# Two of the first four ada_w blocks as rows on TensorE, parameter loads between chunks, gate steps laid out anew, last squares summed on VectorE

## The chip, the cores and the metric

The kernel runs on one core of a Trainium2 chip, all in fp32. The metric is the device time of one execution in microseconds (us), as the median of several runs. The engines are named as in the profile: PE (TensorE matmul), PEld (its weight load), DVE (VectorE), ACT (ScalarE), POOL (GpSimd), SP (SyncE, which only issues DMAs here). An fp32 matmul stands in the trace as two records.

## The reference

One sequence of 256 tokens, width 1024, runs through two layers. Everything is modulated by a vector `c`.

```python
cond = silu(c)
for l in range(2):
    mod = cond @ ada_w[l] + ada_b[l]           # ada_w[l]: 1024 x 9216; nine vectors of 1024
    sh0, sc0, gt0, sh1, sc1, gt1, sh2, sc2, gt2 = split(mod, 9)
    h = rms_norm(x, norm_g[l, 0]) * (1 + sc0) + sh0
    x = x + 0.5 * (1 + gt0) * swiglu(h, ffn_w_in[l, 0], ffn_w_out[l, 0])     # hidden width 2816
    h = rms_norm(x, norm_g[l, 1]) * (1 + sc1) + sh1
    x = x + (1 + gt1) * token_mixer(h, ...)    # RWKV-7 and mLSTM branches of 512 each, two sigmoid gates of 1024
    h = rms_norm(x, norm_g[l, 2]) * (1 + sc2) + sh2
    x = x + 0.5 * (1 + gt2) * swiglu(h, ffn_w_in[l, 1], ffn_w_out[l, 1])
return rms_norm(x, final_g)
```

## The kernel before

The program has five hand-written instruction streams, one for each engine, and each stream is executed in its order. Streams wait for one another through counters: `PE.at(l, "name")` is the count that PE's stream has reached when the step of that name is done, and DV, AC and PO are the same for DVE, ACT and POOL. So the order of the code is the order of the work, and a wait holds up everything behind it on its engine.

**Start.** SP loads `x` and the six units 2 to 7 of the first four column blocks of `ada_w[0]` (512 columns each, a block is two units of 1 MB, `ada_first`, L434); POOL loads units 0 and 1. PE transposes `x`, sums its squares with a matrix of ones, and computes block 1 of `cond @ ada_w` (units 2 and 3) as 32 matmuls with 128x128 weights and one moving column. DVE computes blocks 0, 2 and 3 with eight multiply-adds of 128x512 each, a transpose and a reduction; PE spreads their sums with `ada_columns`. `first_factors` makes shift and scale of them, `modulated` makes `hT` (the normed and modulated input) on DVE and ACT, and the first FFN starts. SP meanwhile loads the weights of the first chunks into a ring of four slots.

**FFN** (`ffn` on every engine). 22 chunks of 128 hidden columns. PE runs up(0), up(1), down(0), up(2), down(1) and so on: `up` makes gate and up products, ACT applies silu, DVE multiplies (`hid`), `down` adds to the output in four PSUM banks. A plain chunk has 16 matmuls of 256 moving columns in `up`. For chunks where `seven()` is true, `up` is a seven-product (Strassen-like) scheme instead: 28 matmuls of 128 columns on sums of weights (`weight_sums`, four 128x512 adds on DVE, made two chunks ahead), and four more DVE additions of the products. All chunks from the third on are such, but for 7, 12 and 17 in layer 0's first FFN. In chunks 2 to 19 DVE also works on the later blocks of `ada_w` (`ada_of_chunk`): 24 units in layer 0's first FFN, each four multiply-adds of 128x512.

**Mixer.** After the projections, PE works on the recurrences in two groups of heads, g = 0 and 1, with long chains of 64x64 matmuls, each step of which waits for a copy on DVE or ACT. Between these, PE takes steps from a list of 128 independent matmuls of 256 columns, the products of the branch gates: `gates(place)` emits as many of them as `GATE_PLACES` gives for that place, and the last 33 are made at "tail", after the recurrences. A sigmoid on ACT follows every 16 steps.

**Second FFN of layer 0.** ACT's stream issues the 20 DMAs of layer 1's parameters (`params_of`) after the modulation of the mixer's output and ahead of the FFN.

**End.** DVE adds the last FFN's output to x in eight pieces. For each quarter b of the channels, PE transposes it with 4 matmuls, and then, when ACT has squared it, sums its squares over the channels with 4 more (one moving column of ones). Root, reciprocal, scaling and four output DMAs follow.

Of the kernel before, what the change touches and what calls it, by code (L numbers as in the profile page):

```python
# [104 lines left out]
GATE_PLACES = (("num", 36), ("masks 0 a", 8), ("masks 0 b", 4), ("inverse 0 a", 2), ("inverse 0 b", 2),  # L105
# [39 lines left out]
def seven(l, half, c):  # L145
    return c >= 2 and not (l == half == 0 and c in (7, 12, 17))
# [64 lines left out]
def trunk(nc, numbers, x_in, c_in, ada_w, ada_b, norm_g, ffn_w_in, ffn_w_out, mix_w_in, rwkv_mu, rwkv_w0,  # L211
          rwkv_w_up, rwkv_a0, rwkv_a_up, rwkv_g_up, rwkv_k_k, rwkv_k_a, rwkv_r_k, rwkv_ln_g, rwkv_ln_b,
          conv_w, conv_b, gate_b, mlstm_ln_g, branch_r, branch_m, w_out, final_g, out):
    with ExitStack() as ctx:
# [186 lines left out]
        def units_summed(u):  # L401


            return u - 1 if u >= 8 else 2
# [160 lines left out]
        def _(ac):  # L565
# [13 lines left out]
            def modulated(l, name):  # L579
# [3 lines left out]
                act(rs[:, :], rs[:, :], ACT.Exp, f"rs {name}", scale=-0.5)  # L583
                for k in (0, 1, 2, 4, 6):
# [29 lines left out]
            def params_of(l):  # L614
# [26 lines left out]
                for dst, src in params:  # L641
                    ac.dma_start(dst, src).then_inc(params_full, 16)  # L642
# [9 lines left out]
            params_of(0)  # L652
            modulated(None, "start")
            for l in range(DEPTH):
# [3 lines left out]
                scaled_ahead(l, "half 0")  # L658
                modulated(l, "half 0")
# [101 lines left out]

                for g in range(2):
                    gates(f"masks {g} a")
# [26 lines left out]
                    gates(f"inverse {g} c")  # L790
                    for n in range(2):
# [7 lines left out]
                    gates(f"y {g} b")  # L799

# [30 lines left out]
        def _(dv):  # L831
# [1157 lines left out]
```

## Time and profile before

| what | value |
|---|---|
| median of 3 runs (all) | 1531.95 us (1531.02, 1531.95, 1535.5) |
| the profiled execution, its own time | 1532.11 us |
| its span, first to last instruction | 1530.4 us |
| PE busy | 1488.9 us, 97% |
| DVE busy | 904.8 us, 59% |
| ACT busy | 262.6 us, 17% |
| mean granted TensorE clock | 0.989 of full |

The busy time of PE is modelled at its ends, so 97% does not say that PE does useful work all the time; gaps between its instructions, and stretches with a lower granted clock, are read from the timeline and the windows. A granted clock of 1.00 is 2.4 GHz and 0.50 is 1.2 GHz; a value between is a mean over a window in which it changed.

### The profile page before, as it was taken

The numbers are of one execution on the slowest core, as the hardware profiler recorded it, in microseconds if no ns is written. First come the engines' busy times: TensorE is split into PE (matmuls) and PEld (weight loads), VectorE is DVE, ScalarE is ACT, GpSimd is POOL, SyncE is SP. The second block draws the span as 40 slices with busy tenths as digits, with TensorE's granted clock in tenths as the row PEclk, the third lists the DMA queues.
The fourth block names the chain that finished last, engine by engine and source line by source line (L and its number), as shares of the span: only waits on it lengthen the run. The fifth ranks groups of instructions, "written<-read, shape, count | busy, mean of one in ns | idle before, by whom it ended". The sixth has DMA issues, their size and how long they took to land.

```text
span 1530.4 us, 27256 instructions
## 1 busy us (share of the span) xinstructions
PE 1488.9 (97%) x11846; PEld 1355.8 (89%) x11846; DVE 904.8 (59%) x1770; ACT 262.6 (17%) x523; POOL 76.3 (5%) x143
## 2 busy tenths in 40 slices
PE   5999999999999998999999999999999999999998
PEld 4899999788888888999989999988888888899998
DVE  5588877554434326888866768665633432655454
ACT  2100002532222020000030000035222200200001
POOL 7001000000000000000000000000000000000000
PEclk7999999999999999999999999999999999999999
DMA  9789997243321575889866878743341247466550
GB/s 333 229 281 307 304 306 221 84 124 97 86 56 57 173 241 162 272 280 288 271 196 216 267 243 271 205 125 124 110 110 30 57 156 243 124 187 189 176 165 28
DMA packets 306231, 282.91 MB, mean 185 GB/s; under 512 B 15368, under 2 KB 269696, under 8 KB 306112
## 3 DMA queue, kind: packets, MB, share of 16 engines
q1 hardware_dynamic: 287168, 211.12, 46.0%
q0 software_dynamic: 17952, 69.21, 13.2%
q8 instruction: 93, 1.52, 0.4%
q10 hardware_dynamic: 992, 0.85, 0.2%
q14 instruction: 26, 0.21, 0.0%
HBM read 280.10 MB, written 1.05 MB: 184 GB/s over the span
## 4 chain that ended last, share of the span: by engine, by line
PE 95%; DVE 2%; DMA 1%; ACT 1%; issue 0%; ACTq 0%; SPq 0%; DVEq 0%
PE ps L1376 94%; DMA arena<-in_ada_w_dram 1%; PE ps L1380 1%; DVE ada_acc L852 1%; ACTq L642 0%; ACT rs L567 0%; DVE y_both L1247 0%; ACT hT L567 0%; DVE hT L883 0%; ACT arena L567 0%; DVE hT L886 0%; SPq L434 0%; DVE arena L1286 0%; DVE ada_turn L858 0%; DVE arena L1281 0%
## 5 line engine op out<-in xcount | busy, mean ns | idle before, releaser
L1376 PE MATMUL ps<-hT,ring 128*128 128x256 f32 (+2 forms) x2768 | 500.2, 336 | 4.8 <-ACT hT L567 4.8
L1376 PEld LDWEIGHTS ps<-hT,ring 128*128 128x128 f32 (+1 forms) x2768 | 436.6, 191 | 61.7 <-issue 10.7
L1376 PE MATMUL ps<-arena,ring 128*128 128x256 f32 (+1 forms) x1568 | 355.5, 381 | 4.4 <-DVE arena L928 4.4
L1376 PEld LDWEIGHTS ps<-arena,ring 128*128 128x128 f32 x1568 | 293.0, 191 | 42.0 <-DVE arena L928 4.8
L1376 PE MATMUL ps<-y_both,arena 128*128 128x128 f32 x1848 | 219.9, 275 | 0.0
L1376 PEld LDWEIGHTS ps<-y_both,arena 128*128 128x128 f32 x1848 | 212.8, 192 | 0.2
L852 DVE SCALAR_TENSOR_TENSOR ada_acc<-ada_stage,cond,ada_acc 128x512 f32<-128x512 f32 x231 | 173.5, 751 | 9.0 <-DMA ada_stage<-in_ada_w_dram 1.1
L1376 PE MATMUL ps<-y_both,ring 128*128 128x128 f32 (+1 forms) x872 | 137.3, 306 | 0.0
L937 DVE TENSOR_TENSOR arena<-arena,ps 128x256 f32<-128x256 f32 x77 | 32.3, 420 | 176.0 <-ACT arena L603 175.9
L1376 PEld LDWEIGHTS ps<-y_both,ring 128*128 128x128 f32 x872 | 123.3, 191 | 6.4
L603 ACT ACTIVATE arena<-ps 128x128 f32<-128x128 f32 x77 | 21.3, 277 | 580.6 <-PE ps L1376 580.6
L494 POOL DMA_DIRECT2D ada_stage<-in_ada_w_dram x66 | 49.6, 751 | 1330.2 <-DVE ada_acc L852 699.5
L1376 PEld LDWEIGHTS ps<-arena 64*64 64x64 f32 (+1 forms) x2880 | 94.0, 136 | 18.5 <-issue 8.1
L1376 PE MATMUL ps<-arena 64*64 64x64 f32 (+3 forms) x2880 | 101.4, 227 | 7.8 <-ACT arena L567 2.8
L1376 PE MATMUL ps<-hT,arena 128*128 128x128 f32 x616 | 81.4, 275 | 0.0
L1376 PEld LDWEIGHTS ps<-hT,arena 128*128 128x128 f32 x616 | 75.0, 192 | 0.0
L567 ACT ACTIVATE arena<-ps 128x256 f32<-128x256 f32 (+4 forms) x96 | 42.7, 468 | 122.0 <-PE ps L1376 95.7
L1008 DVE TENSOR_TENSOR arena<-ring 128x512 f32<-128x512 f32 x77 | 52.8, 686 | 14.5 <-DMA ring<-in_ffn_w_out_dram 14.1
L1376 PE MATMUL ps<-xn,ring 128*128 128x256 f32 x256 | 55.6, 379 | 0.0
L1013 DVE TENSOR_TENSOR arena<-ring,arena 128x512 f32<-128x512 f32 x77 | 53.3, 692 | 2.7
L605 ACT ACTIVATE arena<-arena 128x256 f32<-128x256 f32 x77 | 32.1, 417 | 131.8 <-DVE arena L941 131.8
L1376 PEld LDWEIGHTS ps<-xn,ring 128*128 128x128 f32 x256 | 48.6, 190 | 6.6
(228 smaller groups left out, 1064.6 us busy)
## 6 DMA issues: line engine op xcount, KB each, us to landing
ring<-in_ffn_w_in_dram SPq DMA_DIRECT2D x176, 512.0 KB, 5.3
ada_stage<-in_ada_w_dram POOLq DMA_DIRECT2D x66, 1024.0 KB, 7.2
ring<-in_ffn_w_out_dram SPq DMA_DIRECT2D x88, 512.0 KB, 6.5
ring<-in_mix_w_in_dram SPq DMA_DIRECT2D x46, 512.0 KB, 5.1
ring<-in_mix_w_in_dram SPq DMA_DIRECT2D x12, 1024.0 KB, 5.4
ring<-in_mix_w_in_dram SPq DMA_DIRECT2D x6, 1536.0 KB, 6.4
ring<-in_mix_w_out_dram SPq DMA_DIRECT2D x8, 1024.0 KB, 5.2
arena<-in_ada_w_dram SPq DMA_DIRECT2D x6, 1024.0 KB, 17.9
```

Source lines behind the costliest of these rows:

```text
L494: po.dma_start(ada_stage[:, u % 2], ada_rows(l, col, u % UNITS)).then_inc(ada_full[u % 2], 16)
L567: nc.scalar.activation(out_, in_, func, **kw).then_inc(*AC.step(label))
L603: nc.scalar.activation(parts[:, 7, :], ps[:, base(c), 0:P], ACT.Copy).then_inc(first_copied, 1)
L605: nc.scalar.activation(view(sil[:, c % 2, :], 2, P), parts[:, 0:7:6, :], ACT.Silu)\
L852: V.scalar_tensor_tensor(dst, stage[:, k, :], cond[:, kk_:kk_ + 1], dst, ALU.mult, ALU.add).then_inc(ada_done, 1)
L937: link(l, V.tensor_tensor(parts[:, 0:2, :], parts[:, 7:8, :].broadcast_to([P, 2, P]), both[:, 1:5:3, :], ALU.add))
L1008: V.tensor_tensor(s1, a21, a22, ALU.add).then_inc(w_summed, 1)
L1013: V.tensor_tensor(s4, a12, s2, ALU.subtract).then_inc(w_summed, 1)
L1376: return nc.tensor.matmul(out_, lhsT, rhs, start=start, stop=stop, **kw)
L1380: return nc.tensor.transpose(out_, in_, ident[0:n, 0:n])
```

## The change

1. **Rows.** Block 1 and block 3 are made by PE with `cond` as the weights (one column) and the stage as the moving data: 8 matmuls of 512 columns each (`ada_row`), whose result is one row on one partition. ACT copies the row (`row n`) and four matmuls with one moving column turn it into columns (`row_columns`). DVE makes blocks 0 and 2 alone; it now normalises `x` before it waits for the last block, and reads the sums from PSUM without three copies. On ACT, `root` is split off and comes ahead of the row copies.
2. **Seven everywhere.** Chunks 7, 12 and 17 of layer 0's first FFN use the seven-product form as well.
3. **Parameter loads.** The 20 DMAs of `params_of(1)` are issued two at a time at the start of chunks 2 to 11 of layer 0's second FFN.
4. **Gate steps.** 15 of the 33 steps at "tail" move to six new places: "heads" (4), "uz 0" (2), "y 0 c" (2), "next" (3), "uz 1" (2), "y 1 c" (2). The sigmoids on ACT move with them.
5. **End.** DVE adds the squares of quarters 1, 2 and 3 to those of quarter 0 between its last pieces, and PE sums the result with 4 matmuls instead of 16, ahead of the transposes of the last quarter.

```diff
-GATE_PLACES = (("num", 36), ("masks 0 a", 8), ("masks 0 b", 4), ("inverse 0 a", 2), ("inverse 0 b", 2),
-               ("inverse 0 c", 2), ("y 0 a", 5), ("y 0 b", 4),
+GATE_PLACES = (("num", 36), ("heads", 4), ("masks 0 a", 8), ("masks 0 b", 4), ("inverse 0 a", 2), ("inverse 0 b", 2),
+               ("inverse 0 c", 2), ("uz 0", 2), ("y 0 a", 5), ("y 0 b", 4), ("y 0 c", 2), ("next", 3),
                ("masks 1 a", 8), ("masks 1 b", 4), ("inverse 1 a", 5), ("inverse 1 b", 2),
-               ("inverse 1 c", 4), ("y 1 a", 5), ("y 1 b", 4), ("tail", 33))
+               ("inverse 1 c", 4), ("uz 1", 2), ("y 1 a", 5), ("y 1 b", 4), ("y 1 c", 2), ("tail", 18))
...
 def seven(l, half, c):
-    return c >= 2 and not (l == half == 0 and c in (7, 12, 17))
+    return c >= 2
...
     ACT, in ffn:
+                    if half and l + 1 < DEPTH and c == 2:
+                        ac.wait_ge(*PE.at(l - 1 if l else None, "params next"))
+                        ac.wait_ge(*PE.at(l, "g 1"))
+                    if half and l + 1 < DEPTH and 2 <= c < 2 + N_PARAM_DMAS // 2:
+                        params_of(l + 1, 2 * (c - 2), 2 * (c - 2) + 2)
...
     ACT, after the mixer:
-                if l + 1 < DEPTH:
-                    ac.wait_ge(*PE.at(l - 1 if l else None, "params next"))
-                    ac.wait_ge(*PE.at(l, "g 1"))
-                    params_of(l + 1)
-                else:
+                if l + 1 == DEPTH:
...
     DVE, start:
+            dv.wait_ge(*AC.at(None, "rs start"))
+            for k in range(2):
+                free(V.tensor_tensor(hT[:, k, :], x[:, k, :], rs[:, :], ALU.mult), f"normed start {k}")
...
             dv.wait_ge(*PE.at(None, "ada"))
-            free(V.tensor_copy(mod_next[:, 0:4], ps[:, 5, 0:4]))
-            free(V.tensor_copy(mod_next[:, 4:8], ps[:, 4, 16:20]))
-            free(V.tensor_copy(mod_next[:, 8:16], ps[:, 5, 8:16]))
-            dv.wait_ge(*DV.last())
-            first_factors(None, mod_next[:, 0:16], "start")
-            modulated(None, "start")
+            first_factors(None, ps[:, 5, 0:16], "start")
...
     DVE, end:
+            for b in range(4):
+                residual_part(DEPTH - 1, "half 1", b)
+                for n in ((), (), (1,), (2, 3))[b]:
+                    dv.wait_ge(*AC.at("end", f"squares {n}"))
+                    dv.wait_ge(*DV.last())
+                    free(V.tensor_tensor(hT[:, 0:2, :], hT[:, 0:2, :], hT[:, 2 * n:2 * n + 2, :], ALU.add),
+                         "end squares" if n == 3 else None)
...
     PE, start:
+            def ada_row(n):
+                for k in range(KT):
+                    if k % 4 == 0:
+                        pe.wait_ge(first_full[4 * n + k // 4], 16)
+                    last = mm(ps[0:1, n, :], cond[:, k:k + 1], ada_first[:, 4 * n + k // 4, k % 4, :],
+                              start=(k == 0), stop=(k == KT - 1))
+                last.then_inc(*PE.step(f"row {n}"))
...
-            for i in range(4):
-                for k in range(KT):
-                    stage = ada_first[:, k // 4, k % 4, :]
-                    last = mm(ps[:, 4, 16 + i:17 + i], stage[:, i * P:i * P + P], cond[:, k:k + 1],
-                              start=(i == k == 0), stop=(k == KT - 1), skip_group_check=True)
+            ada_row(0)
             pe.wait_ge(params_full, 16 * N_PARAM_DMAS)
             params("params next", 7)
+            row_columns(0, 4)
             pe.wait_ge(*DV.at(None, "ada 0"))
             ada_columns(5, 0, 0, 1, "ada 0")
-            pe.wait_ge(*DV.at(None, "ada 3"))
-            ada_columns(5, 8, 2, 2, "ada")
+            ada_row(1)
+            pe.wait_ge(*DV.at(None, "ada 2"))
+            ada_columns(5, 8, 2, 1, "ada 2")
+            row_columns(1, 12).then_inc(*PE.step("ada"))
```

The rows below give the instructions in the order in which they stand on an engine. First PE at the start, before, from the sum of squares to the first FFN (`arena` holds `ada_first`, L1376 is the helper that records every matmul):

```order
L1376 MATMUL ps<-hT,ones 128x256 x8
L1376 MATMUL ps<-cond,arena 128x1 x32
L1380 MATMUL ps<-ident,rows_a 128x96
L1380 MATMUL ps<-ident,rows_b 128x87
L1376 MATMUL ps<-ada_red,spread 32x4 x4
L1376 MATMUL ps<-ada_red,spread 32x8 x4
L1376 MATMUL ps<-hT,ring 128x256 x32
```

and of the change (the helper is now L1407):

```order
L1407 MATMUL ps<-hT,ones 128x256 x8
L1407 MATMUL ps<-arena,cond 1x512 x8
L1411 MATMUL ps<-ident,rows_a 128x96
L1411 MATMUL ps<-ident,rows_b 128x87
L1407 MATMUL ps<-ident,xn 128x1 x4
L1407 MATMUL ps<-ada_red,spread 32x4 x4
L1407 MATMUL ps<-arena,cond 1x512 x8
L1407 MATMUL ps<-ada_red,spread 32x4 x4
L1407 MATMUL ps<-ident,xn 128x1 x4
L1407 MATMUL ps<-hT,ring 128x256 x32
```

The 32 matmuls with one moving column became 8 with 512 moving columns, ahead of the parameter transposes; a second set of 8 stands ahead of the last `ada_columns`, and two sets of four turn the rows into columns.

Second, PE in the mixer of group 0, before, from the product "uz 0" (64x128 x16) to the first products of group 1 (on `ring`); `hT,ring` rows are gate steps:

```order
L1376 MATMUL ps<-arena 64x64 x16
L1376 MATMUL ps<-arena 64x128 x16
L1376 MATMUL ps<-arena 64x64 x48
L1376 MATMUL ps<-hT,ring 128x256 x5
L1376 MATMUL ps<-arena 64x64 x36
L1376 MATMUL ps<-hT,ring 128x256 x4
L1376 MATMUL ps<-arena 64x64 x16
L1376 MATMUL ps<-ring 64x128 x32
```

and of the change:

```order
L1407 MATMUL ps<-arena 64x64 x16
L1407 MATMUL ps<-arena 64x128 x16
L1407 MATMUL ps<-hT,ring 128x256 x2
L1407 MATMUL ps<-arena 64x64 x48
L1407 MATMUL ps<-hT,ring 128x256 x5
L1407 MATMUL ps<-arena 64x64 x36
L1407 MATMUL ps<-hT,ring 128x256 x4
L1407 MATMUL ps<-arena 64x64 x4
L1407 MATMUL ps<-hT,ring 128x256 x2
L1407 MATMUL ps<-arena 64x64 x12
L1407 MATMUL ps<-hT,ring 128x256 x3
L1407 MATMUL ps<-ring 64x128 x32
```

Two steps came in behind "uz 0", two within the 16 matmuls of the last chain step, and three ahead of group 1's first products.

Third, ACT between the mixer of layer 0 and the silus of the second FFN (L595 and L602 are the silu of chunk 0), before:

```order
L642 DMA rows_b<-in_mlstm_gate_b_dram 1x4 x2
L642 DMA up_wa<-in_rwkv_w_up_dram 32x512
L642 DMA up_wa<-in_rwkv_a_up_dram 32x512
L642 DMA up_g<-in_rwkv_g_up_dram 96x512
L590 ACT_TABLE_LOAD
L595 ACTIVATE arena<-arena,ahead_c 128x256
```

and of the change:

```order
L567 ACTIVATE hT<-hT,shift_c,scale_c 128x256 x5
L592 ACT_TABLE_LOAD
L602 ACTIVATE arena<-arena,ahead_c 128x256
L615 ACTIVATE arena<-ps 128x256
L649 DMA rows_a<-in_ada_b_dram 72x128
L649 DMA rows_a<-in_norm_g_dram 24x128
L610 ACTIVATE arena<-ps 128x128
L612 ACTIVATE arena<-arena 128x256
```

The DMAs that stood ahead of the table load and the first silu now stand behind the second one, two at a time.

## Rows read from the trace of the kernel before

**Rows 1.** page, part 4: shares of the chain that ended last, by engine.

```profile
PE 95%; DVE 2%; DMA 1%; ACT 1%; issue 0%; ACTq 0%; SPq 0%; DVEq 0%
```

**Rows 2.** waits of PE: who waited for whom, us in total, times, longest.

```profile
PE ps L1376 <- DVE arena L928: 4.4, 1, 4.4
...
PE ps L1376 <- ACT arena L567: 2.8, 4, 0.7
PE ps L1376 <- DVE y_both L1247: 2.8, 2, 1.4
...
PE ps L1376 <- DVE xn L1329: 1.9, 2, 1.0
PE ps L1376 <- DVE arena L1324: 1.6, 4, 0.4
```

**Rows 3.** line L434, the last two of its six DMAs, then the last alone.

```profile
L434 SPq DMA_DIRECT2D arena<-in_ada_w_dram x2: 2520/3286/4052, 9.4 to 13.5; - x2
...
DMA to landing us min/median/max: 17.8/18.4/19.1
...
DMA to landing us min/median/max: 17.8/17.8/17.8
```

**Rows 4.** PE timeline: start, us long, engine, line, tiles, count [idle before <-releaser].

```profile
18.03 10.43 PE L1376 MATMUL ps<-cond,arena 128*128 128x1 f32 x64 [1.18 <-DMA arena<-in_ada_w_dram]
...
37.04 0.30 PE L1376 MATMUL ps<-ada_red,spread 128*32 128x8 f32 x8 [7.95 <-DVE ada_red L859]
39.71 16.96 PE L1376 MATMUL ps<-hT,ring 128*128 128x256 f32 x64 [2.37 <-ACT hT L567]
```

**Rows 5.** windows: busy time by engine, then PEclk, DMA share, GB/s.

```profile
20.00:24.00 4.00, 4.00 (x28) 4.00 (x28) 2.80 (x4) 0.00 (x0) 3.49 (x9) 0.72 1.05 331
...
44.00:48.00 4.00, 4.00 (x16) 3.36 (x16) 0.00 (x0) 0.00 (x0) 0.00 (x0) 0.80 1.14 324
```

**Rows 6.** timeline of PE and windows, projection of layer 0.

```profile
353.43 1.99 PE L1376 MATMUL ps<-arena,ident 4*128 4x256 f32 x8
...
356.00:360.00 4.00, 4.00 (x13) 3.33 (x14) 3.29 (x12) 0.99 (x1) 0.00 (x0) 0.57 0.30 62
```

**Rows 7.** timeline of PE, first FFN: down() of three chunks.

```profile
95.34 3.62 PE L1376 MATMUL ps<-arena,ring 128*128 128x256 f32 x16
...
105.04 3.62 PE L1376 MATMUL ps<-arena,ring 128*128 128x256 f32 x16
...
115.41 3.62 PE L1376 MATMUL ps<-arena,ring 128*128 128x256 f32 x16
```

**Rows 8.** windows and timeline of DVE, first FFN.

```profile
66.80:95.93 29.13, 29.13 (x218) 27.89 (x217) 24.85 (x45) 2.08 (x6) 2.24 (x3) 1.00 0.77 239
...
109.52 0.69 DVE L1008 TENSOR_TENSOR arena<-ring 128x512 f32<-128x512 f32 x1 [2.37 <-DMA ring<-in_ffn_w_out_dram]
```

**Rows 9.** timeline, start of layer 0's second FFN.

```profile
568.77 7.53 PE L1376 MATMUL ps<-hT,ring 128*128 128x256 f32 x32 [0.53 <-ACT hT L567]
...
592.16 2.11 PE L1376 MATMUL ps<-arena,ring 128*128 128x256 f32 x9
...
578.22 1.28 ACT L590 ACT_TABLE_LOAD   x1 [6.56 <-issue]
```

**Rows 10.** timeline of PE, the same place in layer 1.

```profile
1308.44 7.53 PE L1376 MATMUL ps<-hT,ring 128*128 128x256 f32 x32 [0.53 <-ACT hT L567]
...
1325.51 1.68 PE L1376 MATMUL ps<-arena,ring 128*128 128x256 f32 x7
```

**Rows 11.** timeline of PE, a group of two gate steps in the recurrence.

```profile
418.48 1.13 PE L1376 MATMUL ps<-hT,ring 128*128 128x256 f32 x4
419.54 0.68 PE L1376 MATMUL ps<-arena 64*64 64x64 f32 x15
```

**Rows 12.** timeline of ACT and PE, the end.

```profile
1518.48 0.63 ACT L567 ACTIVATE hT<-x 128x512 f32<-128x512 f32 x1 [0.24 <-DVE x L916]
...
1523.62 0.95 PE L1376 MATMUL ps<-ones,hT 128*128 128x1 f32 x8
```

More of the change, by code:

```diff
@@ L401, in units_summed @@
         def units_summed(u):
-            return u - 1 if u >= 8 else 2
+            return u - 3 if u >= 8 else 2
         def unit_landed(u):
@@ L577, in scaled_ahead, with root @@
                 nc.scalar.preload_act_table_set("natural_log_exp_and_others")
-            def modulated(l, name):
+            def root(l, name):
                 ac.wait_ge(*PE.at(l, f"sum {name}"))
@@ L612, in _, with params_of @@
             nc.scalar.preload_act_table_set("natural_log_exp_and_others")
-            def params_of(l):
+            def params_of(l, first=0, end=N_PARAM_DMAS):
                 def rows(src):
@@ L640, in params_of @@
                 assert len(params) == N_PARAM_DMAS
-                for dst, src in params:
+                for dst, src in params[first:end]:
                     ac.dma_start(dst, src).then_inc(params_full, 16)
@@ L652, in _ @@
             params_of(0)
+            root(None, "start")
+            for n in range(2):
+                ac.wait_ge(*PE.at(None, f"row {n}"))
+                act(xn[0:1, n, 0:BLOCK], ps[0:1, n, :], ACT.Copy, f"row {n}")
+            ac.wait_ge(*DV.at(None, "factors start"))
             modulated(None, "start")
@@ L658, in _ @@
                 scaled_ahead(l, "half 0")
+                root(l, "half 0")
                 modulated(l, "half 0")
@@ L814, in _ @@
                     scaled_ahead(l, "half 1")
+                    root(l, "half 1")
                     modulated(l, "half 1")
@@ L909, in ahead, with residual_part @@
                 free(V.tensor_tensor(dst, ps[:, bank, 0:T], rs[:, :], ALU.mult), label)
+            def residual_part(l, name, b):
+                dv.wait_ge(*PE.at(l, f"Y {name} {b}"))
+                for k in (2 * b, 2 * b + 1):
+                    free(V.scalar_tensor_tensor(x[:, k, :], duo(b)[:, k % 2, :], gate_c[:, k:k + 1], x[:, k, :],
+                                                ALU.mult, ALU.add), f"x {name} {b}" if k % 2 else None)
             def residual(l, name):
@@ L1954, in _ @@
                 pe.wait_ge(*DV.at(DEPTH - 1, f"x half 1 {b}"))
+                if b == 3:
+                    pe.wait_ge(*DV.at(DEPTH - 1, "end squares"))
+                    for n in range(2):
+                        for t in range(TT):
+                            last = mm(ps[:, 0, t:t + 1], hT[:, n, t * P:t * P + P], ones[:, 0:1],
+                                      start=(n == t == 0), stop=(n == 1), skip_group_check=True)
+                    last.then_inc(*PE.step("sum"))
                 for k in (2 * b, 2 * b + 1):
@@ L1959, in _ @@
                             last.then_inc(*PE.step(f"x turned {t} {k // 4}"))
-                pe.wait_ge(*AC.at("end", f"squares {b}"))
-                for k in (2 * b, 2 * b + 1):
-                    for t in range(TT):
-                        last = mm(ps[:, 0, t:t + 1], hT[:, k, t * P:t * P + P], ones[:, 0:1],
-                                  start=(k == t == 0), stop=(k == KT - 1), skip_group_check=True)
-            last.then_inc(*PE.step("sum"))
             PE.close()
```

37 lines of the change are left out of this document (28 added, 9 removed).

## The prediction

> **What bounds the kernel now.** The profiled execution took 1532.11 us with a span of 1530.4, so 1.7 lie outside the span; the median of the runs is 1531.95. All sums below are made against this one execution and carried over to the median, 0.16 lower. I read first the page's chain that ended last: PE holds 95% of it [rows 1]. So only three things can shorten the time: fewer or shorter records on PE, gaps in front of PE, and stretches in which PE's clock is at half. The waits of PE [rows 2] show the gaps that one releaser makes; the timeline and windows of the five changed places show the rest.
>
> Of PE's price I use one unit: a plain chunk has 48 records of 256 columns and its period is 10.37 us [rows 7], so a record takes 0.216 at full clock; at half clock it takes 0.432.
>
> **The start.** PE's stream is held by DMA and DVE here, not by its work. It makes block 1, waits 7.95 for DVE's sums until 37.04, then 2.37 for the first `hT`, and the first FFN begins at 39.71 [rows 4]. The granted clock falls to half during the matmuls with one moving column (mean 0.72 in 20:24), and the mean of 0.80 in 44:48 puts the return at 45.6 [rows 5] (0.40 of 4 us at half is 1.6 us): the FFN's first 5.9 us run at half.
>
> In the change a row matmul of 512 columns is two records of 512, so four units of 0.216, 0.86 at full and 1.73 at half. Row 0 needs units 2 and 3 and fits where the old block 1 stood. Row 1 needs units 6 and 7. The last two of L434's DMAs are issued at 9.4 and 13.5 and the last lands 17.8 later, at 31.3, the one before it 19.1 later, at 28.5 [rows 3]. Its first four matmuls begin at 28.5, and the last four begin at 31.3 or when the first four are done. At full clock the end is 31.3 + 4 x 0.863 = 34.8. With the first 5.9 us at half, as in the FFN, 3.4 of the eight are done by 34.4 and the other 4.6 take 4.0: 38.4. I take the middle, 36.6, and 0.3 for the small matmuls between. Behind it: a copy on ACT (0.63 as for 128x512 [rows 12], less on one partition), four tiny matmuls, and the stretch of 2.67 from 37.04 to 39.71 less three copies on DVE and the first normalisation, which are now done ahead (estimate 0.7). That is 36.9 + 0.6 + 2.0 = 39.5, as good as before. But PE has just streamed 8 x 512 columns, and if that brings the clock back as the FFN's matmuls do, the FFN starts at full clock: 2.95 less at half. Of this some 0.35 goes to `hT`'s eight pieces, which ACT and DVE deliver one by one and which now hold a faster PE (an estimate, one piece's delay). Term: **-2.6**; bounds +5.2 (below) and -4.3 (row 1 at full clock throughout, 1.7 earlier).
>
> Whether a row matmul, whose weights are a single column, raises the clock is not shown by any row. The nearest one speaks against it: eight records with four-row weights keep PE busy from 353.43, PE is busy 4.00 of 4.00 us in 356:360, and yet the mean clock there is 0.57 [rows 6]. The rule in the Trainium skill, "TensorE: Matmul & The Clock Gate", Part 1, is that the gate follows how busy PE has been recently and that activity releases the throttle. By that rule alone the row matmuls, which keep PE busy, would warm the clock.
>
> By rows 6 a busy PE with a mostly empty array may stay at half, and the term is +5.2. Against taking those rows over: few of the array's rows carried data there; here all 128 do, and few columns. I keep -2.6, and give +5.2 its chance below.
>
> **Seven everywhere.** down(4), down(5) and down(6) start at 95.34, 105.04 and 115.41 [rows 7]: the first period holds up() of a seven chunk, 9.70, the second that of plain chunk 7, 10.37. Three chunks change: 3 x 0.67 = **-2.0**, if DVE keeps up. For such a chunk DVE gets the four adds of 128x512 of the weight sums, 0.69 each [rows 8], 2.8 together, and four narrower ones of the products, 4.0 to 4.5 in all. In the three seven chunks of 66.80:95.93 DVE is busy 24.85 of 29.13 [rows 8]: 1.43 spare for each. So an unbroken row of seven chunks holds, but the plain chunk in which DVE could catch up is gone, and DVE's waits for weights in the ring, up to 2.37 at a time [rows 8], have only that spare to go into. Bounds: -2.0, and, with a longest wait in each of the three chunks and in its two neighbours, nine in all, 9 x (2.37 - 1.43) - 2.0 = +6.5. I take -2.0, since no wait for DVE in these chunks is among PE's large ones [rows 2].
>
> **Parameter loads.** From the first up() to down(0) layer 0 takes 568.77 to 592.16, 23.39 us; the same work in layer 1, where ACT has no DMAs to issue, 1308.44 to 1325.51, 17.07 [rows 9, 10]. ACT's table load comes 6.56 us of issuing late, at 578.22 [rows 9], so `silu` of chunk 0 is late, PE stands idle, and its clock falls. Term: **-6.3**. In the change, two issues at a time stand ahead of the silu of a chunk: 6.56/20 = 0.33 each, 0.66, on an engine that is busy 17% of the time, and behind an up() of 7 us that covers it. Nothing waits for these parameters before the end of the FFN. Bounds: -6.3, and -5 if the delay shows in one or two of the ten chunks.
>
> **Gate steps.** PE's waits in the mixer at the new places are, over both layers, 2.8 for ACT's copies at L567 (4 waits), 2.8 for y_both (2), 1.9 for xn (2) and 1.6 for L1324 (4): 9.1 us in 12 waits [rows 2]. Two gate steps in such a place take 1.06 from 418.48 to 419.54, against 4 x 0.216 = 0.86 [rows 11]: 0.2 for changing over. 15 steps in a layer are 30 records, 6.5 us, so 13 us of work stand against 9.1 of gap: enough to fill them. Term: -(9.1 - 12 x 0.2) = **-6.7**. "tail" shrinks from 33 steps, 14.2 us, to 18, 7.8; it covers DVE's and ACT's last work on group 1, for which PE shows no wait now [rows 2], and what of the 6.5 us less is not spare comes back there. The sigmoids that move add table loads on ACT, 1.28 each [rows 9], in a recurrence where ACT also feeds PE. Bounds: -9.1 and 0.
>
> **The end.** Now the squares of the last quarter are done on ACT at 1518.48 + 0.63 = 1519.11, and PE ends its sums at 1524.57 [rows 12], since 8 records of sums per quarter, 0.95, and the transposes queue up. In the change one add of 0.69 stands ahead of DVE's last piece: squares at 1519.8; another add, 1520.5; 4 matmuls of 0.95, 1521.5. That is 3.1 less, of which up to 0.4 goes to the last transposes, now behind the sums while root and reciprocal run. Term: **-2.8**, bounds -1.5 and -3.1.
>
> **Sum.** -2.6 - 2.0 - 6.3 - 6.7 - 2.8 = -20.4; 1532.1 - 20.4 = **1511.7**. One thing is loose by itself: after the four-row matmuls the clock fell to half for some us [rows 6], and where it falls there may shift with everything ahead; +-1.7.
>
> **Rivals.**
> *The clock stays at half for the rows.* For: rows 6, and the fall during one-column work in 20:24 [rows 5]. Then PE reaches row 1 at half and its 8 matmuls take 13.8 us: 28.5 + 13.8 = 42.3; the FFN begins at 44.9, 5.2 late, and still runs 5.9 us at half. The start gives +5.2 in place of -2.6: 1519.5 (1518.6 if hT's pieces hide in it). Chance 0.28.
> *DVE passes its waits on in the first FFN* , halfway to the upper bound (-2.0 + 8.5 / 2): 1516.0. For: no chunk left to catch up in. Against: 1.43 spare in each. Chance 0.11.
> *The gate steps fill nothing*: what they cover is found again behind the shorter tail, or the chains move with them: 1511.7 + 6.7 = 1518.4. For: tail loses 6.5 us a layer. Against: PE shows no wait behind it now. Chance 0.06.
> *DVE becomes the bound of the whole first FFN*, slower: DVE is busy 8.28 a chunk, and if it waits for the ring twice in each chunk, at 2.37, a chunk takes 13.0 against 9.70, over 18 chunks +60: 1573. It ends slower by 0.3% from waits of 2.7 us in each chunk on (8.28 + 2.7 - 9.70 = 1.3; 18 x 1.3 = 23, against -18.4 of the other terms). Against: 2.37 is the longest wait, and DMA share is 0.77 [rows 8]. Chance 0.03. That the time stays within 0.3% needs two of these at once; 0.02.
>
> **How the numbers follow.** My forecast has 0.50, its own range 1508.5 to 1514.5 (end +1.3, clock at 356 +-1.7, row 1 at full clock -1.7). With the first three rivals, 0.95 lies below 1521; a range of 8 in 10 and more is 1508 to 1520.5. 0.3%, or 4.6 us, is about what a measurement of this kernel can tell from no change. All cases but the last two lie beyond it: faster 0.94, same 0.03, slower 0.03.
>
> **What would show it.** In the profile of the changed kernel: the granted clock is 1.00 when the first FFN begins, at 39 to 40; if it is 0.50 and the row matmuls take 1.7 each, the first rival holds. All down() periods from chunk 3 on are 9.70. From the first up() to down(0) of layer 0's second FFN, 17 us, as in layer 1. PE's waits for y_both, xn and L1324 fall from 9.1 to under 2.5, with no new wait behind the last gate step. PE's last sums end some 3 us nearer to the last squares. The prediction is wrong if any of these fails, and most if PE's waits for `hid` (DVE) grow in the first FFN.

## The result, and the profile of the changed kernel

The changed kernel takes 1511.92 us as the median of four runs (1510.17 to 1516.2), beside 1531.49 for the kernel before on the same chip. The ratio is 0.987, with a 95% interval of 0.984 to 0.989: faster, by 1.3%. Its profiled execution took 1511.64 us with a span of 1509.9; the one of before took 1532.11 with 1530.4, so the spans differ by 20.5 us. The forecast was 1511.7, 20.4 below before.

PE still holds the chain that ended last, less exclusively than before [rows 1]. Page of the changed kernel, part 4:

```profile
PE 92%; DVE 3%; DMA 3%; SPq 1%; ACT 1%; issue 1%; ACTq 0%; DVEq 0%
```

Waits of PE (who waited for whom: us in total, times, longest), to be held against [rows 2]:

```profile
PE ps L1407 <- ACT hT L567: 5.1, 7, 1.3
...
PE ps L1407 <- DVE arena L971: 1.2, 2, 0.7
```

The waits for y_both, xn, L1324 (now L1347) and the copies at L567 are gone. The two for DVE's line L971, which makes `hid` (the product of the up products and silu that `down()` reads), are new.

The start, timeline of PE (start, us long, engine, line, tiles, rows*columns of the weights, shape of the moving operand, count, idle time before and its releaser), as [rows 4] before:

```profile
15.10 7.03 PE L1407 MATMUL ps<-arena,cond 128*1 128x512 f32 x16
...
27.84 7.97 PE L1407 MATMUL ps<-arena,cond 128*1 128x512 f32 x15 [2.42 <-DMA arena<-in_ada_w_dram]
...
36.92 1.05 PE L1407 MATMUL ps<-ident,xn 1*128 1x1 f32 x8 [0.64 <-ACT xn L567]
39.30 14.11 PE L1407 MATMUL ps<-hT,ring 128*128 128x256 f32 x64 [1.33 <-ACT hT L567]
```

and windows there (busy time by engine, then granted clock, DMA share, GB/s):

```profile
24.00:28.00 4.00, 1.58 (x19) 1.30 (x20) 2.78 (x4) 0.00 (x0) 3.47 (x9) 0.90 1.05 388
28.00:32.00 4.00, 4.00 (x7) 0.64 (x6) 3.86 (x11) 0.00 (x0) 3.33 (x11) 0.67 1.15 319
...
36.00:40.00 4.00, 2.03 (x14) 1.67 (x13) 1.53 (x7) 2.03 (x4) 0.00 (x0) 1.00 1.11 355
```

The first two lines are row 0 and row 1, whose weights have one column (128*1). The clock fell in the pause between them (0.90, then 0.67), came back during row 1, and was 1.00 when the first FFN began at 39.30, where before it was 0.50 until 45.6. The FFN's first products take 14.11 us in place of 16.96 [rows 4].

Since every chunk of both kernels has one `down()` that waits for `hid`, its starts give a ruler: the difference after minus before at the same `down()` says how much has been gained up to there.

| up to | difference, us | term | measured | forecast |
|---|---|---|---|---|
| first down(), layer 0 | -3.27 | start | -3.3 | -2.6 |
| end of the first FFN | -3.65 | seven everywhere | -0.4 | -2.0 |
| end of layer 0's mixer | -9.21 | gate steps, layer 0 | -5.6 | |
| second down() of layer 0's second FFN | -15.53 | parameter loads | -6.3 | -6.3 |
| layer 1's first FFN | -15.53 | nothing changed there | 0.0 | 0 |
| end of layer 1's mixer | -17.85 | gate steps, layer 1 | -2.3 | (both) -6.7 |
| end of the span | -20.48 | end | -2.6 | -2.8 |

In the two lines of gate steps the clock's fall behind the four-row matmuls is included; it is taken out below. Within the first FFN the difference grows by 0.65 at each of the three chunks and reaches -5.23, and then PE waits twice. Timeline of PE, changed kernel:

```profile
218.94 3.72 PE L1407 MATMUL ps<-arena,ring 128*128 128x256 f32 x16 [0.52 <-DVE arena L971]
...
246.37 0.36 PE L1407 MATMUL ps<-ada_red,spread 128*32 128x48 f32 x8 [0.72 <-DVE arena L971]
```

The second FFN of layer 0, PE and then ACT, as [rows 9] before:

```profile
559.56 7.53 PE L1407 MATMUL ps<-hT,ring 128*128 128x256 f32 x32 [0.53 <-ACT hT L567]
...
576.63 3.62 PE L1407 MATMUL ps<-arena,ring 128*128 128x256 f32 x16
```

```profile
562.47 1.28 ACT L592 ACT_TABLE_LOAD   x1
...
567.12 0.38 ACT L615 ACTIVATE arena<-ps 128x256 f32<-128x256 f32 x1 [2.85 <-PE ps L1407]
...
576.83 0.28 ACT L610 ACTIVATE arena<-ps 128x128 f32<-128x128 f32 x1 [9.32 <-PE ps L1407]
```

From the up() at 559.56 to the second down() (the rows that the forecast compared, and called down(0)) it is 17.07 us, which is [rows 10] to the hundredth. ACT loads its table at 562.47, with no DMA issue ahead of it.

The end, PE and DVE, as [rows 12] before:

```profile
1503.06 1.02 PE L1407 MATMUL ps<-ones,hT 128*128 128x1 f32 x8 [0.70 <-DVE hT L1392]
```

```profile
1499.84 0.69 DVE L1392 TENSOR_TENSOR hT<-hT 128x512 f32<-128x512 f32 x1
...
1501.42 1.49 DVE L1392 TENSOR_TENSOR hT<-hT 128x512 f32<-128x512 f32 x2
```

And the place behind the projection's four-row matmuls, windows of the changed kernel, for [rows 6]:

```profile
356.00:360.00 4.00, 4.00 (x20) 3.51 (x20) 3.71 (x9) 1.63 (x2) 0.00 (x0) 1.00 0.72 186
1080.00:1084.00 4.00, 4.00 (x21) 3.53 (x20) 1.29 (x6) 0.00 (x0) 0.00 (x0) 0.74 0.02 4
1084.00:1088.00 4.00, 4.00 (x17) 3.42 (x16) 3.79 (x12) 2.34 (x2) 0.00 (x0) 0.83 0.84 223
```

In the kernel before the clock fell there in layer 0 and not in layer 1; in the changed one it is the other way round. The price of a fall can be read from the 32 records behind the four-row matmuls, which are the same work in both layers and both kernels. Timeline of PE, the kernel before (layer 0, layer 1) and then the changed one:

```profile
356.42 8.75 PE L1376 MATMUL ps<-ring,hT 128*128 128x256 f32 x32
...
1097.80 7.17 PE L1376 MATMUL ps<-ring,hT 128*128 128x256 f32 x32
```

```profile
352.71 7.17 PE L1407 MATMUL ps<-ring,hT 128*128 128x256 f32 x32
...
1082.50 8.57 PE L1407 MATMUL ps<-ring,hT 128*128 128x256 f32 x32
```

The next products start at 365.01 and 1104.81 before, at 359.72 and 1090.91 in the changed kernel. So up to there the ruler goes from -3.65 to -5.29 in layer 0 (the fall that only the kernel before has, 1.64) and from -15.53 to -13.90 in layer 1 (the fall that only the changed one has, 1.63). From there to the end of the mixer it goes down by 3.92 in layer 0 and by 3.95 in layer 1: that is what the gate steps gain, 7.9 together.

### The profile page after: what moved, and what is told of

The parts are those of the page before. It is cut to its first block, busy times and chain, and to the rows that moved or that the text cites. A ratio compares the mean times of both kernels' runs of the same rounds, so it can differ in the third digit from the quotient of the medians.

```text
span 1509.9 us, 27350 instructions
## 1 busy us (share of the span) xinstructions
PE 1486.1 (98%) x11878; PEld 1342.4 (89%) x11878; DVE 910.6 (60%) x1784; ACT 269.6 (18%) x532; POOL 74.8 (5%) x143
## 4 chain that ended last, share of the span: by engine, by line
PE 92%; DVE 3%; DMA 3%; SPq 1%; ACT 1%; issue 1%; ACTq 0%; DVEq 0%
PE ps L1407 92%; DMA ring<-in_ffn_w_out_dram 1%; DMA arena<-in_ada_w_dram 1%; DVE ada_acc L868 1%; PE ps L1411 1%; SPq L434 1%; ACT rs L567 0%; ACT hT L567 0%; DVE x L930 0%; DVE arena L1027 0%; DVE arena L1030 0%; DVE arena L1028 0%; DVE hT L899 0%; DVE ada_turn L874 0%; DVE arena L971 0%
## 5 line engine op out<-in xcount | busy, mean ns | idle before, releaser
L1407 PE MATMUL ps<-hT,ring 128*128 128x256 f32 (+2 forms) x2720 | 485.0, 332 | 3.8 <-ACT hT L567 3.8
L1407 PEld LDWEIGHTS ps<-hT,ring 128*128 128x128 f32 (+1 forms) x2720 | 420.9, 190 | 58.2 <-issue 10.3
L1407 PE MATMUL ps<-arena,ring 128*128 128x256 f32 (+1 forms) x1568 | 353.8, 379 | 0.5 <-DVE arena L971 0.5
L1407 PEld LDWEIGHTS ps<-arena,ring 128*128 128x128 f32 x1568 | 291.7, 190 | 37.4 <-DVE arena L971 0.7
L1407 PE MATMUL ps<-y_both,arena 128*128 128x128 f32 x1920 | 228.5, 275 | 0.0
L1407 PEld LDWEIGHTS ps<-y_both,arena 128*128 128x128 f32 x1920 | 221.1, 192 | 0.2
L1407 PE MATMUL ps<-y_both,ring 128*128 128x128 f32 (+1 forms) x896 | 140.4, 305 | 0.0
L1407 PEld LDWEIGHTS ps<-y_both,ring 128*128 128x128 f32 x896 | 126.2, 191 | 6.4
L1407 PEld LDWEIGHTS ps<-arena 64*64 64x64 f32 (+1 forms) x2880 | 94.2, 136 | 12.7 <-issue 9.7
L1407 PE MATMUL ps<-arena 64*64 64x64 f32 (+3 forms) x2880 | 101.5, 227 | 0.8 <-DVE arena L1304 0.6
L1407 PE MATMUL ps<-hT,arena 128*128 128x128 f32 x640 | 84.5, 275 | 0.0
L1407 PEld LDWEIGHTS ps<-hT,arena 128*128 128x128 f32 x640 | 77.9, 192 | 0.0
L1027 DVE TENSOR_TENSOR arena<-ring 128x512 f32<-128x512 f32 x80 | 54.9, 686 | 16.6 <-DMA ring<-in_ffn_w_out_dram 16.4
L567 ACT ACTIVATE arena<-ps 128x256 f32<-128x256 f32 (+4 forms) x96 | 42.7, 468 | 102.1 <-PE ps L1407 100.6
L1407 PE MATMUL ps<-xn,ring 128*128 128x256 f32 x256 | 55.6, 379 | 0.0
L1028 DVE TENSOR_TENSOR arena<-ring 128x512 f32<-128x512 f32 x80 | 54.8, 685 | 0.0
```

The source lines that it names most:

```text
L567: nc.scalar.activation(out_, in_, func, **kw).then_inc(*AC.step(label))
L1027: V.tensor_tensor(s1, a21, a22, ALU.add).then_inc(w_summed, 1)
L1028: V.tensor_tensor(s3, a11, a21, ALU.subtract).then_inc(w_summed, 1)
L1407: return nc.tensor.matmul(out_, lhsT, rhs, start=start, stop=stop, **kw)
```

## The experiments

The theory: the sum holds by its terms, and where a term is off, the clock and the transfers move it. Rival: the agreement is real only for the total of this trace, and the terms for start and chunks come out otherwise in other executions. Twelve kernels ran, each beside the kernel before on its chip. "Ruler" is the difference of the `down()` starts against the trace of before.

### What brings the clock back

Four kernels, one for each loop below, put extra matmuls, whose result nothing uses, into the kernel before, where PE otherwise waits from 29 to 37 us. The names in the comments are those of the kernels; each kernel has the wait and one of the loops:

```diff
             ada_columns(5, 0, 0, 1, "ada 0")
+            pe.wait_ge(*AC.at(None, "x 0 1"))
+            for k in range(4):                  # d_rows: one-column weights, 512 moving columns
+                mm(ps[0:1, 0, :], cond[:, k:k + 1], ada_first[:, 0, k, :])
+            for k in range(18):                 # d_cols: 128x128 weights, one moving column
+                mm(ps[:, 0, 0:1], ada_first[:, 0, k % 4, 0:P], cond[:, k % 8:k % 8 + 1])
+            for k in range(4):                  # d_four: four rows, 512 moving columns
+                mm(ps[:, 0, :], ada_first[0:4, 0, 0, 0:P], ada_first[0:4, 0, k, :])
+            for k in range(4):                  # d_full: 128x128 weights, 512 moving columns
+                mm(ps[:, 0, :], ada_first[:, 0, 0, 0:P], ada_first[:, 0, k, :])
```

**d_rows.** 

> The kernel before with four extra row matmuls (one-column weights, 512 moving columns; their result is not used) behind the first ada_columns at about 29 us, where PE otherwise waits until 37. Theory A (row matmuls are work that brings the clock back, as in the changed kernel, where the granted clock was 0.67 in 28:32 and 1.00 in 32:36): the granted clock is 1.00 by about 36 and the first FFN, whose first products took 16.96 us, takes about 14.1; its start stays at 39.7; the time falls by about 2.9 us to 1529. Theory B (the changed kernel kept its clock only because it never had the one-moving-column matmuls, and rows do not raise it): the clock stays 0.50 until 45, the first products take 17 us, time unchanged.

**d_cols.** 

> The kernel before with 18 extra matmuls with 128x128 weights and one moving column (result not used) at the same place as in d_rows. Both theories: these matmuls, under which the clock fell in 20:24, keep it at 0.50 while PE is listed as busy, so the first FFN's products take 17 us again. If they raise the clock as well, any busy PE does, and the fall in 20:24 has another cause.

**d_four.** 

> The kernel before with four extra matmuls of 512 columns over four rows only (128 columns of weights, result not used) at the same place. If few rows are what let the clock fall behind the four-row matmuls of the projection (mean 0.57 in 356:360 of the kernel before, 0.74 in 1080:1084 of the changed one), the clock stays at 0.50 and the first products take 17 us. If the moving columns alone count, it is 1.00 by 36 and they take 14.1.

**d_full.** 

> The control: four extra matmuls of 512 columns over all 128 rows and 128 columns of weights at the same place (result not used). Both theories: the clock is 1.00 by 36, the first products take 14.1 us, the time falls by 2.9 us. If not, the place and length of the insertion do not allow the test.

Measured: timeline of PE (the extra matmuls, then the first FFN) and windows 32:36 and 40:44, kernel by kernel. d_rows:

```profile
27.83 6.14 PE L1376 MATMUL ps<-arena,cond 128*1 128x512 f32 x8
...
39.49 15.89 PE L1376 MATMUL ps<-hT,ring 128*128 128x256 f32 x64 [2.37 <-ACT hT L567]
```

```profile
32.00:36.00 4.00, 1.97 (x4) 0.26 (x2) 3.75 (x6) 0.00 (x0) 3.71 (x6) 0.88 1.13 327
...
40.00:44.00 4.00, 4.00 (x12) 3.22 (x11) 2.13 (x5) 2.81 (x4) 0.00 (x0) 0.60 1.03 375
```

d_full, the control:

```profile
28.14 5.87 PE L1376 MATMUL ps<-arena 128*128 128x512 f32 x8
...
39.62 15.61 PE L1376 MATMUL ps<-hT,ring 128*128 128x256 f32 x64 [2.42 <-ACT hT L567]
```

```profile
32.00:36.00 4.00, 2.00 (x4) 0.43 (x3) 3.75 (x6) 0.00 (x0) 3.28 (x6) 0.93 1.13 329
...
40.00:44.00 4.00, 4.00 (x13) 3.24 (x13) 2.25 (x5) 2.94 (x4) 0.00 (x0) 0.65 1.03 389
```

d_cols:

```profile
30.03 7.84 PE L1376 MATMUL ps<-cond,arena 128*128 128x1 f32 x36
...
40.26 16.17 PE L1376 MATMUL ps<-hT,ring 128*128 128x256 f32 x64 [2.17 <-ACT hT L567]
```

```profile
32.00:36.00 4.00, 4.00 (x20) 4.00 (x21) 3.75 (x6) 0.00 (x0) 3.43 (x6) 0.50 1.13 328
...
40.00:44.00 4.00, 3.74 (x9) 3.05 (x10) 2.86 (x6) 3.13 (x6) 0.00 (x0) 0.50 1.03 387
```

d_four:

```profile
32.45 7.19 PE L1376 MATMUL ps<-arena 4*128 4x512 f32 x8
...
42.03 17.07 PE L1376 MATMUL ps<-hT,ring 128*128 128x256 f32 x64 [2.16 <-ACT hT L567]
```

```profile
32.00:36.00 4.00, 4.00 (x14) 1.72 (x14) 3.75 (x6) 0.00 (x0) 3.77 (x6) 0.50 1.13 329
...
40.00:44.00 4.00, 1.97 (x5) 1.64 (x6) 3.82 (x14) 2.18 (x4) 0.00 (x0) 0.50 1.04 385
```

The third number from the right is the granted clock. With row matmuls it is 0.88 in 32:36, with full ones 0.93; with one moving column and with four rows it stays at 0.50, although PE is listed as busy for 4.00 of the 4.00 us. So here row matmuls, with all 128 rows and one column of weights, brought the clock back as full ones did, and matmuls over four rows did not. What I had expected of the time did not come: PE then idles for 2.9 and 2.4 us, the clock falls again (0.60 and 0.65 in 40:44), and the first down() is only 1.29 and 1.45 us earlier instead of 2.9. The control falls short in the same way, so the kind of matmul is not the reason; that it is the pause is likely, but no run without the pause was made here. The four times (1536.36, 1537.53, 1535.01 and 1532.51 in this order, before 1537.93) are single runs and say nothing here: in d_rows, d_cols and d_full the clock fell behind the four-row matmuls of layer 1, where it did not in the trace of before (3.3 us each by the ruler), and d_rows and d_cols lost 2.05 and 1.17 us more in the first FFN, in waits for DVE that the next part comes back to.

### Seven everywhere

```diff
 def seven(l, half, c):
-    return c >= 2
+    return c >= 2 and not (l == half == 0 and c in (7, 12, 17))   # u_seven
+    return c >= 2 and not (l == half == 0 and c == 12)            # v_seven12
...
-ADA_FIRST, ADA_END = 2, 20
+ADA_FIRST, ADA_END = 1, 20                                        # v_first1
```

**u_seven.** 

> The changed kernel with chunks 7, 12 and 17 plain again. Theory A (the three chunks saved PE 1.85 us but took away the chunks in which DVE caught up, and its lateness gave 1.49 back as two waits near 218 and 246 us): the waits are gone, the first FFN is longer by only 0.4 us. Rival B (the waits come from the earlier start of the FFN against the transfers, not from the seven-product chunks): the waits stay and the FFN is 1.9 us longer.

**v_seven12.** 

> The changed kernel with chunk 12 alone plain. Theory A: one chunk for DVE to catch up is enough, both waits (0.7 and 0.8 us at 218 and 246) go, PE pays 0.6: the first FFN is 0.9 us shorter than in the changed kernel. Rival B: 0.6 longer.

**v_first1.** 

> The changed kernel with DVE's ada_w units spread over 19 chunks, from chunk 1 on, in place of 18 from chunk 2 on (in all four FFNs). Chunk 1 had a margin of 8.6 us between hid and down. Theory A (DVE's accumulated lateness makes the waits): the waits go and nothing is paid on PE, the first FFN is 1.5 us shorter. Rival C (DVE is late because transfers land late, here DMA share is 0.97 from 95 us on): the earlier units only move the transfers, and half or less is gained.

**again.** 

> The changed kernel unaltered, once more, beside the variants. In the traces so far kernels with the same start began the first FFN at 37.5, 39.0, 39.3 and 40.6 us, with a granted clock at row 1 of 1.00, 0.72, 0.67 and 0.50. If that spread is chance of the clock and of the transfers and not of the edits, this trace shows another of these values and a time between 1509 and 1516.

Measured, by the ruler from the first down() to the end of the first FFN (0 is what the kernel before needs):

| kernel | first FFN | start | time, us (runs) |
|---|---|---|---|
| changed kernel, first trace | -0.38 | -3.27 | 1511.9 |
| again | +2.95 | -3.13 | 1513.9 (4) |
| u_gates, same FFN | -1.53 | -3.60 | 1520.6 (4) |
| v_warm, same FFN | -0.84 | -3.41 | 1512.5 (4) |
| v_two, same FFN | +0.48 | -0.20 | 1521.5 (1) |
| u_seven | 0.00 | -5.06 | 1510.3 (4) |
| v_seven12 | -1.31 | -0.45 | 1515.5 (4) |
| v_first1 | -1.96 | -3.60 | 1513.4 (4) |
| v_warm_first1, same FFN as v_first1 | -1.80 | -3.26 | 1512.6 (4) |

u_seven has none of the waits, and its first FFN is 0.4 us longer than that of the changed kernel's first trace, as theory A says; v_seven12 has none either and is 0.9 shorter; v_first1 has none and is 1.6 shorter. Rival B (the waits come from the earlier start) would have kept them in u_seven, whose FFN started earliest of all. But each of these is one trace, and the kernels of the clock test show that the waits don't need the change. They have chunks 7, 12 and 17 plain, and in two of the four PE waits for DVE at `last_sums` (the place in the last up() where PE spreads DVE's sums) all the same: 1.10 us in d_cols, and in d_rows

```profile
250.78 0.36 PE L1376 MATMUL ps<-ada_red,spread 128*32 128x48 f32 x8 [1.55 <-DVE arena L952]
```

So each seven chunk saves its 0.65, and DVE's lateness gives back an amount that changes from one execution to the next: something in all five traces with no plain chunk and DVE's units as in the change, something in two of the six with three plain chunks (before, the four of the clock test, u_seven), next to nothing in the two with the earlier units (0 and 0.15). In `again` it gives back more than all, in two waits, 0.82 ahead of a down() and 1.93 at `last_sums`, behind which the clock fell:

```profile
248.20 0.36 PE L1407 MATMUL ps<-ada_red,spread 128*32 128x48 f32 x8 [1.93 <-DVE arena L971]
```

```profile
212.00:250.00 38.00, 35.26 (x271) 33.45 (x270) 32.26 (x62) 2.50 (x7) 2.25 (x3) 1.00 0.90 267
248.00:252.00 4.00, 3.80 (x29) 3.67 (x30) 0.74 (x6) 0.00 (x0) 0.00 (x0) 0.71 0.54 146
```

In v_first1 the same stretch has no gap on PE, with less work left on DVE (31.00 against 32.26 us), because one unit of ada_w is done in chunk 1:

```profile
212.00:250.00 38.00, 38.00 (x291) 36.23 (x290) 31.00 (x62) 3.19 (x9) 1.50 (x3) 1.00 0.85 248
```

Five traces of the same FFN give -1.53, -0.84, -0.38, +0.48 and +2.95, a mean of +0.1; the six with three plain chunks give 0 four times, +1.17 and +2.05, a mean of +0.5. So three more seven chunks are worth nothing measurable as the change makes them, and about -1.9 in both traces in which DVE's units begin one chunk earlier. The times don't tell these kernels apart: the ratios to before are 0.986 (u_seven), 0.989 (v_seven12) and 0.988 (v_first1), with intervals that overlap that of the changed kernel.

The unaltered kernel's own spread (`again`): its FFN begins at 39.44 with a clock of 0.59 in 28:32, one more value in the row as expected; its four times are 1511.88 to 1518.44, the last one that of the trace and 2.4 above the range that I had given.

### Start: filling the pause

```diff
             ada_row(0)
+            for k in range(2):
+                mm(ps[0:1, 1, :], cond[:, k:k + 1], ada_first[:, 0, k, :])
             pe.wait_ge(params_full, 16 * N_PARAM_DMAS)
...
             ada_columns(5, 0, 0, 1, "ada 0")
+            for k in range(2):
+                mm(ps[0:1, 1, :], cond[:, k:k + 1], ada_first[:, 0, k, :])
```

v_warm_first1 has this and `ADA_FIRST = 1`.

**v_warm.** 

> The changed kernel with four more row matmuls whose result is not used, two behind row 0 and two behind the first ada_columns, in the time in which PE waits for transfers between 22 and 28 us. Theory A (the clock falls in that gap because PE rests, and row 1 then runs at half until it has raised the clock again): the clock is 1.00 throughout 24:36, row 1 ends at 34.3 and the first FFN begins at 37.5 to 38, 1.5 to 3 us sooner than in the changed kernel. Rival B (row 1's end is set by the landing of unit 7, the clock does not matter): no sooner than 39.

**v_warm_first1.** 

> The edits of v_warm and v_first1 together: first FFN begins at 37.5 to 38, no waits in it for DVE, so its end is 1.5 to 3 us (start) and 0.4 to 1.6 us (waits) sooner than in the changed kernel: 1509 to 1507 where the changed kernel takes 1512. What the clock does behind the four-row matmuls, 1.5 to 3.4 us for each fall, may hide this in a single trace; if the medians do not differ from the changed kernel's by more than their interval, that is what was lost in.

Timeline of PE (row 1 but for its last records, first FFN) and windows of v_warm:

```profile
27.71 6.60 PE L1407 MATMUL ps<-arena,cond 128*1 128x512 f32 x15 [0.35 <-DMA arena<-in_ada_w_dram]
...
37.78 15.48 PE L1407 MATMUL ps<-hT,ring 128*128 128x256 f32 x64 [1.33 <-ACT hT L567]
```

```profile
28.00:32.00 4.00, 4.00 (x11) 0.76 (x10) 3.86 (x11) 0.00 (x0) 3.33 (x11) 1.00 1.15 317
...
36.00:40.00 4.00, 2.67 (x10) 2.22 (x10) 1.53 (x7) 2.94 (x6) 0.00 (x0) 0.66 1.10 353
```

Half of it came. The clock is 1.00 through row 1 and the FFN begins at 37.78, 1.5 us sooner. But then PE waits between row 1 and the FFN, as in the changed kernel, and this time the clock falls there (0.66 in 36:40); the first products take 15.48 in place of 14.11, and the first down() is at -3.41, where it was at -3.27. The pause that costs the clock has moved from one side of row 1 to the other. v_warm_first1 does the same (37.68, 15.74), and the 1507 to 1509 us expected of it did not come. Beside `again` (ratio to before 0.9876, interval 0.9854 to 0.9898) v_warm has 0.9868 (0.9847 to 0.9888) and v_warm_first1 0.9861 (0.9842 to 0.9879): neither is shown to be better.

### Gate steps and parameter loads

u_gates has the old `GATE_PLACES` in the changed kernel, 33 steps at "tail". v_two moves the steps of "y 0 c" and "y 1 c" to "tail", and apart from that issues all 20 DMAs at chunk 2:

```diff
-    ("y 0 c", 2), ... ("y 1 c", 2), ("tail", 18))
+    ("y 0 c", 0), ... ("y 1 c", 0), ("tail", 22))
...
                     if half and l + 1 < DEPTH and c == 2:
                         ac.wait_ge(*PE.at(l - 1 if l else None, "params next"))
                         ac.wait_ge(*PE.at(l, "g 1"))
-                    if half and l + 1 < DEPTH and 2 <= c < 2 + N_PARAM_DMAS // 2:
-                        params_of(l + 1, 2 * (c - 2), 2 * (c - 2) + 2)
+                        params_of(l + 1)
```

**u_gates.** 

> The changed kernel with the gate steps laid out as before (33 at the tail). From the two traces the mixers with new places were shorter by 7.9 us in sum, with one fall of the clock behind the four-row matmuls in each trace. Theory A: longer by 7.9, in the twelve waits of before. Rival B: part of the 7.9 comes from elsewhere (clock, other work), and it is longer by 6.7 or less.

**v_two.** 

> Two edits of the changed kernel at places far apart, each read from the timeline. First, all 20 DMAs of the parameters are issued at once at the start of chunk 2 of layer 0's second FFN. Theory A (what counted was only that they stood ahead of chunk 0's silu): ACT is idle 9.3 us there and the issues take 7, so nothing changes. Rival B (more than two at a time delay the silu): PE waits for chunk 2, some us. Second, the two gate steps at y 0 c and y 1 c go back to the tail (22 there). Theory A (a switch costs 0.26, a filled wait is worth 0.56 by start-to-start times): each layer's mixer is 0.6 us longer; rival C (the switch costs what the wait did): no difference.

u_gates: its mixers come out as those of before by the ruler, -0.12 in layer 0 and +0.01 in layer 1, with the clock's falls where before has them. So the changed kernel's -5.6 and -2.3, -7.9 together, come from the gate steps and from where the clock fell, and from nothing else. The waits of before are back, to the tenth:

```profile
PE ps L1407 <- ACT arena L567: 2.8, 4, 0.7
PE ps L1407 <- DVE y_both L1270: 2.8, 2, 1.4
...
PE ps L1407 <- DVE xn L1352: 1.9, 2, 1.0
...
PE ps L1407 <- DVE arena L1347: 1.6, 4, 0.4
```

The time is 1520.6; the two medians, of different chips, differ by 8.6.

v_two, parameter loads: ACT issues the 20 DMAs in one go, the last one at 583.65 (the copies of chunk 2 wait for PE until 586.48, behind 9.32 us of idle time):

```profile
583.65 1.35 ACTq L648 DMA_DIRECT2D up_g<-in_rwkv_g_up_dram  x1
586.48 0.28 ACT L609 ACTIVATE arena<-ps 128x128 f32<-128x128 f32 x1 [9.32 <-PE ps L1406]
```

The ruler goes down by 6.33 over this stretch; in the eight traces with two DMAs at a time by 6.32 or 6.33. So it was the place, behind the first two silus, and not the two at a time.

v_two, gate steps: layer 1's mixer, without a fall of the clock, gains 2.12 instead of the changed kernel's 3.95. That is 1.8 lost, not 0.6. Two steps fewer ahead of "uz 1" let the 16th step of a group, and with it a sigmoid and its table load on ACT, fall into another place, and the copy of "uz 1" comes late. Timeline of PE, layer 1:

```profile
1214.60 1.91 PE L1406 MATMUL ps<-arena 64*64 64x64 f32 x96 [1.23 <-ACT arena L567]
```

Held against the changed kernel record by record, this place costs 1.30 and each of the two emptied places 0.26 (a wait of 0.56 by start-to-start times, less a switch): 1.8. Layer 0 has the same wait of 1.23 at 482.82 and loses 0.55 more at a wait of 0.33 (488.66) for which the trace names no releaser.

## Why the prediction was right, point by point

**Start, -2.6 against -3.3 in this trace.** Row 1 began at 27.84 (28.5 forecast), and the FFN at 39.30 (39.5). The rival with a clock at half for all the rows did not come, and two experiments fit that: matmuls with one-column weights brought the clock back (d_rows), matmuls over four rows did not (d_four), so [rows 6] was the wrong neighbour to fear. The estimate of 0.35 for `hT`'s pieces was too high: there is one wait of 1.33 ahead of the FFN and none in it. But the term is no constant. Over the seven traces whose start is that of the change it is -5.06, -3.60, -3.60, -3.27, -3.13, -0.45 and -0.20, mean -2.8. In these the FFN begins between 37.5 and 40.6, with a clock between 0.50 and 1.00 in 28:32. Row 1 at full clock came once in these (u_seven), and gave 0.8 more than my bound of -4.3. The other bound, +5.2 with row 1 at half throughout, was never met: where the clock was lowest (v_seven12, 0.50 in 28:32) it was already 0.81 in 32:36, and the term is -0.45. The forecast of the mean was right; that the first trace lay near it is luck.

**Seven everywhere, -2.0 against -0.4.** This step failed. The saving of the three chunks is there (0.65 each, 0.67 forecast), but "if DVE keeps up" was taken as given since an unbroken stretch early in the FFN showed 1.43 us spare for each chunk [rows 8]. That stretch was read before the transfers grow dense (DMA share 0.77; it is 0.96 to 0.98 from 95 us to 212 in the changed kernel, and 0.94 to 0.98 in the kernel before, where it could have been seen). From 95 to 212 DVE is busy 34.7 to 34.8 of every 39 us (31.2 to 32.0 before), which leaves it 1.04 to 1.07 a chunk and not 1.43; its waits for the ring go on (11.4 us in the whole FFN), and its margin to `down()` shrinks from 4.6 to 0.1. By the prediction's own list of signs (all down() periods 9.70, no growing waits for `hid`) this part of it is wrong. The mean of five traces, +0.1, lies halfway between the term and the rival "DVE passes its waits on" (+2.25, chance 0.11), and one trace, `again`, went beyond that rival. That the change causes these waits alone is not shown: d_rows and d_cols had them without it.

**Gate steps, -6.7 against -7.9.** A term mis-sized in its first factor: I counted the idle time of the twelve waits, 9.1. From start to start each wait holds PE up by 0.16 more than its idle time says (0.56 where idle is 0.40), 11.0 in all. The steps gain 3.92 in layer 0 and 3.95 in layer 1, 7.9 of these 11.0, so that a switch costs 0.26 and not the 0.2 read from [rows 11]. Nothing came back behind the shorter tail.

**Parameter loads, -6.3 against -6.3**, and **end, -2.8 against -2.6**: here each step went as worked out. At the end DVE's second add waits for the squares and the pair takes 1.49, so PE's sums start 0.7 after its last transposes and end at 1504.08.

**The total.** 0.1 us of agreement is more than the working deserves: the start gave 0.7 and the gate steps 1.2 more, seven everywhere 1.6 less, and the clock's fall behind the four-row matmuls happened once in each trace, so that it cancelled. I had allowed 1.7 either way for it, and one fall cost 1.6. In 14 traces (28 places) it fell 20 times; where it lasted longer it cost 3.3 (layer 1 of d_rows, where nothing else differs in the mixer), and with a wait behind it 4.5 (v_seven12, layer 1). That alone can move an execution by as much as an edit here gains.

## What to carry to other kernels

Read the spare time of a helper engine where the kernel is at its tightest, not in the first clean stretch: a chunk that looks slow on the bottleneck engine may be the one in which the helper catches up. Take the price of a short wait on PE from start to start, and expect the switch to a filler to cost something too (0.26 us here against waits of 0.56 to 1.54); and when steps are taken out of a numbered list, look where the work of other engines that is tied to their numbers ends up. Here a run of 20 DMA issues on a compute engine cost 6.3 us ahead of the first work that others wait for, and nothing behind it.

## What the runs showed of the hardware

A matmul with a single column of weights and 512 moving columns brought the granted clock from 0.50 to 0.88 in 32:36, close to one with 128 columns of weights (0.93); one over four rows, with PE busy 4.00 of 4.00 us, left it at 0.50, and so did one moving column. At the start the clock was lost again around short waits: in the changed kernel before row 1 (a wait of 2.42 us, 0.67 in 28:32), in v_warm behind row 1 (waits of 0.64 and 1.33 with small matmuls between, 0.66 in 36:40). In the changed kernel and in u_seven the same waits behind row 1 left it at 1.00 in 36:40. Whether it falls behind the four-row matmuls is not decided by the kernel: `again` is the changed kernel unaltered, and there it fell in both layers, in the first trace in one.
